# The end of a chunked scan: the last gate projection is moved ahead, output-projection units fill between the last head's steps, and its copies go to ScalarE

## What is computed

```python
def hgrn2_mixer(h, s0, lb, w_in, b_f, g_norm_w, w_out):
    q, f, i, z = jnp.split(h @ w_in, ...)
    q = silu(q); f = lb + (1 - lb) * sigmoid(f + b_f)
    logf = log(f); k = 1 - f; v = i
    o, S = hgrn2_scan(q, k, v, logf, s0)      # S_t = diag(f_t) S_{t-1} + k_t v_t^T, o_t = S_t^T q_t
    o = rmsnorm(o, g_norm_w)                  # over the 256 values of a head
    y = (o * silu(z)) @ w_out                 # the output projection
    return y, S
# and around it: x = x + gate * y
```

## Time and profile before

| | us |
|---|---|
| median of 3 runs | 1130.75 |
| lowest, highest | 1126.59, 1130.91 |
| profiled execution, its own time | 1128.67 |
| its span, first to last instruction | 1127.1 |
| PE busy | 1090.7 (97%) |
| DVE, ACT busy | 633.3 (56%), 506.0 (45%) |

### The profile page before, as it was taken

One profiled execution on the slowest core, in us unless ns is written; L12 is line 12 of the kernel. 1 busy time (PEld: TensorE's weight loads), 2 busy tenths in 40 slices (PEclk: granted clock), 3 DMA queues, 4 the chain that ended last, 5 costly groups with the idle time before them and its releaser, 6 DMA issues.

```text
span 1127.1 us, 26213 instructions
## 1 busy us (share of the span) xinstructions
PE 1090.7 (97%) x11141; PEld 1041.8 (92%) x11141; DVE 633.3 (56%) x1278; ACT 506.0 (45%) x1026; POOL 151.0 (13%) x156
## 2 busy tenths in 40 slices
PE   8999999999999999889998999999999999999998
PEld 6799999999999999779997999999999999998997
DVE  4776675858585758683435734552465246437332
ACT  4653444535444444641113554563465265447122
POOL 1000000000000000000000640252045006300000
PEclk9999999999999999999998999999999999999999
DMA  9864445444453535226224346424723652262541
GB/s 325 285 195 126 144 130 153 127 144 136 134 149 120 151 118 151 80 70 207 76 75 140 99 124 154 111 72 112 181 79 89 154 141 76 63 155 77 161 116 43
DMA packets 232218, 147.73 MB, mean 131 GB/s; under 512 B 7875, under 2 KB 226205, under 8 KB 231590
## 3 DMA queue, kind: packets, MB, share of 16 engines
q1 hardware_dynamic: 217456, 134.17, 41.9%
q10 hardware_dynamic: 14646, 11.89, 3.1%
HBM read 124.00 MB, written 22.02 MB: 130 GB/s over the span
## 4 chain that ended last, share of the span: by engine, by line
PE 79%; DVE 11%; ACT 4%; issue 3%; DMA 2%; SPq 1%; DVEq 0%; ACTq 0%
PE PJ L380 26%; PE PJ L1576 18%; PE PJ L1291 15%; PE PJ L401 2%; DVE dd L952 2%; PE X L1692 1%; PE X L1269 1%; PE X L1164 1%; PE PJ L1601 1%; PE X L1719 1%; PE PJ L624 1%; DVE atd L922 1%; PE X L1271 1%; DMA pre<-in_ada_w_dram 1%; PE X L1192 1%
## 5 line engine op out<-in xcount | busy, mean ns | idle before, releaser
L353 DVE TENSOR_TENSOR w_lo<-raw,w_hi 128x1024 fp32r<-128x1024 f32 (+1 forms) x128 | 157.0, 1240 | 178.8 <-ACT w_hi L345 169.9
L345 ACT ACTIVATE w_hi<-raw 128x1024 fp32r<-128x1024 f32 (+1 forms) x128 | 129.2, 1025 | 155.3 <-PE PJ L1576 69.9
L1576 PE MATMUL PJ<-w_hi,h_hi 128*128 128x256 f32 x600 | 167.3, 287 | 0.7 <-DVE w_lo L353 0.7
L1576 PE MATMUL PJ<-w_lo,h_hi 128*128 128x256 f32 x600 | 164.6, 283 | 0.0
L380 PE MATMUL PJ<-h_hi,w_hi 128*128 128x288 f32 (+1 forms) x736 | 160.7, 300 | 0.6 <-ACT v_ L874 0.6
L380 PE MATMUL PJ<-h_hi,w_lo 128*128 128x288 f32 (+1 forms) x736 | 157.7, 296 | 0.0
L380 PE MATMUL PJ<-h_lo,w_hi 128*128 128x288 f32 (+1 forms) x736 | 157.4, 295 | 0.0
L1576 PE MATMUL PJ<-w_hi,h_lo 128*128 128x256 f32 x480 | 135.8, 283 | 0.0
L380 PEld LDWEIGHTS PJ<-h_hi,w_hi 128*128 128x128 f32 x736 | 118.1, 189 | 4.3 <-issue 2.8
L380 PEld LDWEIGHTS PJ<-h_hi,w_lo 128*128 128x128 f32 x736 | 118.9, 189 | 0.0
L380 PEld LDWEIGHTS PJ<-h_lo,w_hi 128*128 128x128 f32 x736 | 118.8, 189 | 0.0
(11 more groups left out here) (329 smaller groups left out, 2165.7 us busy)
## 6 DMA issues: line engine op xcount, KB each, us to landing
raw<-in_a_w_in_dram SPq DMA_DIRECT2D x48, 512.0 KB, 4.9
raw<-in_ada_w_dram SPq DMA_DIRECT2D x32, 512.0 KB, 3.8
raw<-in_b_w_in_dram SPq DMA_DIRECT2D x64, 256.0 KB, 3.6
kvc<-in_cache_kv_w_dram SPq DMA_DIRECT2D x24, 512.0 KB, 5.8
pre<-in_ada_w_dram SPq DMA_DIRECT2D x16, 512.0 KB, 10.0
s<-in_state_hgrn_dram SPq DMA_DIRECT2D x8, 1024.0 KB, 8.4
out_hgrn_sample_dram<-s ACTq DMA_DIRECT2D x8, 1024.0 KB, 5.0
raw<-in_a_w_out_dram SPq DMA_DIRECT2D x16, 512.0 KB, 4.7
```

What stands on the lines that cost most here:

```text
L345: act.activation(w_hi[:, i % SPLITS, 0:size], raw[:, n % RAWS, 0:size], ACT.Copy).then_inc(hi_done, 1)
L353: dve.tensor_tensor(w_lo[:, i % SPLITS, 0:size], raw[:, n % RAWS, 0:size], w_hi[:, i % SPLITS, 0:size].bitcast(F32), ALU.subtract).then_in ...
L1576: last = pe.matmul(PJ[:, tile // 2, tile % 2 * 256:tile % 2 * 256 + 256], a, b[:, k, :], start=(first and k == 0 and i == 0), stop=(kk == ...
```

## The change

It touches heads 0 to 6 only in how waits and reads are worded (`pe_states` is cut into `pe_seq_rows`, `pe_chunk_states` and `pe_seq_out`, in the same order; some waits ask for less). The rest is at the end of the scan:

- PE, step 7: `project_T(ticket_w(7, 5), ...)` runs whole, after the new states and ahead of the output products of head 6.
- PE, step 8: the turning of the conditioning rows comes first, then units 0 and 1, `pe_mean(6)`, and units 2 to 7 one by one between the scan's parts. The chunk states come ahead of the sequences' rows.
- PE, step 9: units 8 and 9 ahead of `pe_mean(7)`, units 10 to 13 behind it, then units 0 to 7 of output block 1, then units 14 and 15 of block 0, and units 8 to 15 of block 1.
- ACT takes over eight copies of the last head (`at` from `X` and from `atd`, `sc`), under the new counter `at_done`. Its `oz_hi` copies are spread over steps 7, 8 and 9, and the `split_hi` of the three first output pieces is moved: two into step 7, ("out0", 1, 0) to the very end of step 8.
- DVE: the `oz_lo` are spread likewise, and the `split_lo` of ("out0", 1, 0) stands at the end of step 8, ahead of `oz_lo(8, 14)` of step 9.
- The transposed keys of the short sequences of the last head go to bank 2 of `X` in place of bank 1.

```diff
@@ act_step
             if h == AH:
-                for key in FIRST_OUT0[0:2]:
-                    split_hi(key)
+                oz_hi(4, 6)
             if end:
-                logs_and_exps()
+                if h <= AH:
+                    logs_and_exps()
...
             if h == AH:
-                z_sigmoid(AH - 1, 1)
-                split_hi(FIRST_OUT0[2])
-                oz_hi(0, 10)
+                oz_hi(6, 8)
+                act.wait_ge(gram_ready, 3 * g + 3)
+                act.wait_ge(op_ready, g)
+                for i in (6, 7):
+                    for s0_, s1_, t0_, t1_ in level_blocks(i):
+                        ins = act.activation(at[s0_:s1_, :, t0_:t1_], wide_at(i)[s0_:s1_], ACT.Copy)
+                ins.then_inc(at_done, 1)
...
+                if h == AH:
+                    act.wait_ge(up_ready, g + 1)
+                    act.wait_ge(sp_out, 16 * g)
+                    act.activation(sc[:, 0], X[:, 0, 0:ADV], ACT.Copy).then_inc(at_done, 1)
...
-                for j in range(2 if h < AH - 1 else 1):
+                for j in range(2):
                     z_sigmoid(h, j)
                     ahead(7 + j)
+                    if h == AH - 1 and j == 0:
+                        for key in FIRST_OUT0[0:2]:
+                            split_hi(key)
+            if h == AH - 1:
+                oz_hi(0, 4)
             if h == AH:
-                oz_hi(10, 14)
+                act.wait_ge(gram_read, 3 * g + 2)
+                for q in range(4):
+                    r = slice(BL * q, BL * q + BL)
+                    ins = act.activation(at[r, :, r], atd[r, 0:CH], ACT.Copy)
+                ins.then_inc(at_done, 1)
+                oz_hi(8, 10)
...
                 act.activation(sq0[:, :, TP:T], os_[:], ACT.Square).then_inc(sq_done, 1)
+                if h == AH:
+                    oz_hi(10, 14)
+                    split_hi(FIRST_OUT0[2])
@@ dve_step
             if h == AH:
-                for key in FIRST_OUT0[0:2]:
-                    split_lo(key)
+                z_gate(AH - 1, 1)
+                oz_lo(0, 4)
+                read_ada_chunk(chain, 3 + h)
+                oz_lo(4, 6)
             if h > AH:
-                oz_lo(4, 13)
+                oz_lo(8, 14)
...
-            if h == AH:
-                z_gate(AH - 1, 1)
-                split_lo(FIRST_OUT0[2])
             if h > AH:
-                oz_lo(13, 16)
+                oz_lo(14, 16)
...
             if scan and not new:
                 gram()
                 gram()
-                oz_lo(0, 2)
-                read_ada_chunk(chain, 3 + h)
                 masked_keys()
-                oz_lo(2, 4)
...
+            if h == AH:
+                oz_lo(6, 8)
...
                 new_states((0, 1), ub_read)
+            if h == AH - 1:
+                for key in FIRST_OUT0[0:2]:
+                    split_lo(key)
+            if h == AH:
+                split_lo(FIRST_OUT0[2])
@@ pe_step
             if h == AH:
-                late = (ticket_w(AH - 1, 5), ("w", AH - 1, 5))
-                project_T(*late, range(0, 4))
+                wait_read(pe, ticket_w(AH - 1, 5))
+                turn_ada_groups(3 + h)
+                out0_units(2)
                 pe_mean(pe, f)
-                project_T(*late, range(4, KD))
+                out0_units(3)
+                pe_grams(pe, g, 0)
+                out0_units(4)
+                pe_grams(pe, g, 1)
+                pe_grams(pe, g, 2)
+                out0_units(5)
+                pe_turn_keys(pe, g)
+                out0_units(6)
+                pe_chunk_states(pe, g)
+                pe_seq_rows(pe, g)
+                out0_units(7)
+                pe_seq_out(pe, g)
             if h > AH:
-                out0_units(4)
+                out0_units(10)
                 pe_mean(pe, f)
+                out0_units(14)
+                pe.wait_ge(ada_done, 4 + AH)
+                pe_out(pe, "out0", 1, range(8))
...
             if new:
                 pe.wait_ge(adr_done, 5 + h)
-                if h < AH - 1:
-                    project_T(ticket_w(h, 5), ("w", h, 5))
+                project_T(ticket_w(h, 5), ("w", h, 5), range(KD))
             elif scan:
-                out0_units(2)
+                out0_units(8)
             if scan:
                 pe.wait_ge(ua_read, g + 1)
+                if h == AH:
+                    pe.wait_ge(at_done, 3)
@@ the PE program, after the steps
             out0_units(16)
-            pe.wait_ge(ada_done, 4 + AH)
             for m in range(1, KD):
-                pe_out(pe, "out0", m, range(16))
+                pe_out(pe, "out0", m, range(8 if m == 1 else 0, 16))
```

More of the change, by code:

```diff
@@ L928, in dve_gram @@
                     dve.wait_ge(op_ready, g)
-                for q in range(4):
-                    r = slice(BL * q, BL * q + BL)
-                    dve.tensor_copy(at[r, :, r], atd[r, 0:CH])
+                if g < AH - 1:
+                    for q in range(4):
+                        r = slice(BL * q, BL * q + BL)
+                        dve.tensor_copy(at[r, :, r], atd[r, 0:CH])
                 for x in range(2):
                     r = slice(BL * x, BL * x + BL)
-                    dve.tensor_copy(atz[r, x], atd[r, CH])
-                for i in (6, 7):
+                    ins = dve.tensor_copy(atz[r, x], atd[r, CH])
+                for i in (6, 7) if g < AH - 1 else ():
                     for s0_, s1_, t0_, t1_ in level_blocks(i):
@@ L1048, in dve_step @@
                     dve.wait_ge(sp_out, 16 * g)
-                chain(dve.tensor_copy(sc[:, 0], X[:, 0, 0:ADV]))
+                if h < AH:
+                    chain(dve.tensor_copy(sc[:, 0], X[:, 0, 0:ADV]))
+                else:
+                    dve.wait_ge(at_done, 2)
                 for c in range(1, CH):
@@ L1119, in pe_grams @@
             if group == 2 and g >= 1:
-                pe.wait_ge(fin_done, 2 * g)
+                pe.wait_ge(fin_done, 2 * g - 1)
             for i in range(3 * group, min(3 * group + 3, 8)):
@@ L1138, in pe_turn_keys, with pe_turn_seq_keys, seq_keys_at, pe_seq_rows @@
         def pe_turn_keys(pe, g):
-            pe.wait_ge(gram_read, 3 * g + 3)
             pe.wait_ge(lv_done, XS * g + XS)
+            if g:
+                pe.wait_ge(fin_done, 2 * g)
             for c in range(CH):
                 pe.transpose(X[:, 3, c * P:(c + 1) * P], kh[:, c * P:(c + 1) * P], ident[:])
-            pe.transpose(X[:, 1, 0:P], kh[:, TP:T + TS], ident[:]).then_inc(kt_ready, 1)
-        def pe_states(pe, g):
+            pe_turn_seq_keys(pe, g)
+        def pe_turn_seq_keys(pe, g):
+            bank, c0 = seq_keys_at(g)
+            if g < AH - 1:
+                pe.wait_ge(gram_read, 3 * g + 2)
+            else:
+                pe.wait_ge(at_done, 1)
+            pe.transpose(X[:, bank, c0:c0 + P], kh[:, TP:T + TS], ident[:]).then_inc(kt_ready, 1)
+        def seq_keys_at(g):
+            return (1, 0) if g < AH - 1 else (2, 384)
+        def pe_seq_rows(pe, g):
             b = g % 2
+            pe.wait_ge(gram_read, 3 * g + 3)
+            if g == AH - 1:
+                pe.wait_ge(kz_done, g + 1)
             pe.wait_ge(vs_done, g + 1)
@@ L1234, in pe_step @@
                              lambda c: PJ[:, c // 2, c % 2 * ADV:(c % 2 + 1) * ADV], between)
-            elif h == AH:
-                grams(0)
-                grams(1)
-                wait_read(pe, ticket_w(AH - 1, 5))
-                turn_ada_groups(3 + h)
-                grams(2)
-            if scan:
-                if new:
-                    pe.wait_ge(ada_done, 4 + h)
+            if scan and new:
+                pe.wait_ge(ada_done, 4 + h)
                 pe_turn_keys(pe, g)
@@ L1247, in pe_step @@
                 project_ada(19 + 4 * h, 3)
-            if scan:
-                pe_states(pe, g)
+            if scan and new:
+                pe_seq_rows(pe, g)
+                pe_chunk_states(pe, g)
+                pe_seq_out(pe, g)
             if new:
@@ L1255, in pe_step @@
                 pe.wait_ge(up_read, g + 1)
-                pe.wait_ge(vs_done, g + 1)
+                pe.wait_ge(kz_done, g + 1)
                 pe_new_states(pe, g)
```

13 lines of the change are left out of this document (10 added, 3 removed).

## The result

| | before | after |
|---|---|---|
| median of 5 runs, us | 1130.75 | 1136.42 |
| lowest, highest | 1126.59, 1131.21 | 1135.22, 1136.93 |
| profiled execution, its own time | 1128.67 | 1136.00 |
| its span | 1127.1 | 1134.4 |

The ratio of after to before is 1.0052, with a 95% interval of 1.0035 to 1.0070. The change makes the kernel slower by half a percent; the 0.5% within which I had called two times the same lies inside the interval. Between the two profiled executions it is 7.3 us.

The account below looks back on a forecast made before the run. PE, 97% busy, was taken as bound at the scan's end by the chain through the parked input's read. PE resuming at 522.5 against 515.4, plus 1.8 clock, adds 8.9 to 1128.67: 1137.6, given as 1137.5 us, range 1131.0 to 1141.5.

Parts of the forecast that it names:

- issue gap: PE's unexplained stop within the last head's small matmuls: 2.24 us before, 1.4 us left with one unit put in between.
- wait ahead of unit 6: PE waits some 1.4 us for DVE's low part of block 6, made behind the chain for the new states.
- from there to unit 8: From PE issuing its last output product to unit 8: 7.0 us of squares, copies and splits in series on ACT and DVE.
- clock's price, first gap: Behind the gap between products and unit 8, PE runs at the lower clock: 1.59 to 2.3 us, taken as 1.8.
- from read to PE: From the start of the read of the parked input to PE resuming: 11.5 us, as in the trace of before.
- PE's wait there: Ahead of block 1's second half, PE waits 5.7 us, where it waited 0.69 us before.
- clock's price, second gap: Behind PE's wait ahead of block 1's second half, the clock falls again and costs 1.8 us.
- The stall: Between the products and unit 8, PE has nothing else to do for 7.0 us, which delays the read.
- In-order engines: ACT and DVE take instructions strictly in order, so low parts of blocks 8 and 9 can't pass the waiting piece.
- Heads 0 to 6: These heads gain 0, as none of their reworded waits stood in a gap.
- first rival: PE isn't held behind the products: resumes at 512.3, 1125.6 to 1127.4 us, say 1126.5; chance 0.11.
- third rival: All gaps close and the read costs nothing: 11 us gained, 1117.5 us; chance 0.05.

Follow-up runs that it names:

- e1_split_early: Changed kernel with the high and low part of piece (out0, 1, 0) made in the middle of step 8, not behind the products: 1128.49 us.
- e5_before_lo_early: Kernel before with DVE's wait for the read put behind the low part of piece (out0, 1, 1): 1130.61 us.
- e4_projection_alone: Kernel before with only the last gate projection, its sigmoid and gate moved whole into step 7: 1131.92 us.
- e2_fill_gap: Changed kernel with 48 matmuls of unused results on PE between the last head's products and unit 8: 1135.33 us.
- e3_lo_before_read: Changed kernel with DVE's wait for the read put behind the low part of piece (out0, 1, 1): 1133.50 us.
- e7_two_of_three: Changed kernel with piece (out0, 1, 0) split early and DVE's wait for the read behind the low part of (out0, 1, 1): 1125.53 us.
- e9_no_unit_between: Changed kernel with unit 3 moved from between the last head's first two groups of small matmuls to behind both: 1138.35 us, one run.
- e10_more_order: Changed kernel: e7_two_of_three's edits, units 14 and 15 inside block 1, units 3 and 4 between small-matmul groups, DVE's low parts of blocks 6 and 7 earlier: 1120.37 us.

## Why the prediction was right

The forecast was 1137.5 us, with a shift of 8.9 us on the profiled execution; the measured median is 1136.42 and the shift between the profiled executions 7.3 us. By its steps:

| step | said | measured |
|---|---|---|
| small matmuls start | 472.9 | 472.82 |
| issue gap | 1.4 | 1.26 |
| wait ahead of unit 6 | 1.4 | 1.37 |
| products issued | 493.0 | 493.2 |
| from there to unit 8 | 7.0 | 6.9 |
| unit 8 starts | 500.0 | 500.11 |
| clock's price, first gap | 1.8 | 1.34 |
| read starts | 511.0 | 510.63 |
| from read to PE | 11.5 | 10.17 |
| second half of block 1 | 522.5 | 520.80 |
| PE's wait there | 5.7 | 4.14 |
| clock's price, second gap | 1.8 | 1.2 |

**The stall** is the forecast's main step, and it holds in kind and size: e1_split_early takes it away by moving nothing but the piece. **In-order engines**: DVE's `w_lo` stood in front of `oz_low` and nothing passed it, though the inputs of two blocks were ready (489.46) and DVE was idle for 6.55 us. The rule that I had weighed against the trace says just this, that VectorE takes its instructions strictly in order (the Trainium skill, TensorE: Matmul & The Clock Gate, section Architectural detail: the array is 16× 32×32, not 1× 128×128); by that rule, the trace agrees, with 6.71 us. **Heads 0 to 6** got nothing, as said: the last matmuls ahead of the first changed place start at 456.64, against 456.63. **The issue gap**: the step 2.24 - 0.8 = 1.4 is right in kind, but that it came out at 1.26 is partly luck. The same order of matmuls gave 0.98 us in three of six traces, and with no unit in between it was 2.24, 1.88 and 1.37 us in before, e5_before_lo_early and e4_projection_alone.

**The absolute number** is nearer than the shift. The forecast added 8.9 us to the profiled execution of before, which was 2.1 us under the median; the medians differ by 5.7 us only, and the profiled executions by 7.3. That 1137.5 came within 1.1 us of 1136.42 owes that much to the base.

Three terms were too large, and together make up the 2.3 us by which the shift at the end of block 1 fell short (the sum for the residual starts at 528.55, against 521.91: 6.6 us, for 8.9; the other 0.7 us between the profiled executions came later and isn't explained). The read and what follows it took 10.17 us, since the read itself was 8.81 us and not the 10.16 of the earlier trace rows; I had taken one transfer's time as if it couldn't vary. The first clock's price was taken between 1.59 and 2.3 us and is 1.34 (e2_fill_gap), as only 3.02 us were run at the lower level; in e3_lo_before_read it was 0.8 us more behind the same gap, so the term varies between executions as the read does. The second: eight units take 528.55 - 520.80 = 7.75 us against 521.91 - 515.40 = 6.51, 1.2 us.

**What I had not seen.** That the second gap has two owners. I wrote that the high part of ("out0", 1, 1) "comes in time", which is true of after (516.75, with the read landing at 519.4) but hid that without the read 2.5 us would remain (e3_lo_before_read, e7_two_of_three): the change had put all of PE's cover ahead of the end of block 0. The first rival is what e1_split_early made: I had PE resume at 512.3 there, and it did at 512.26. But that is luck: the read started at 502.15 and not at 500.8 (the issue gap had stayed, with 0.98 us), and PE resumed 10.1 us later and not 11.5. The time was 1128.49 (1127.08 in the profiled execution) and not 1126.5; the clock's price, 1.5 us here, had gone into it only by half. The third rival I gave 0.05, since it "needs the read to be off the chain"; it couldn't be had by this change, but three moves more came nearer to its 1117.5, with 1121.74, and two further ones with 1120.37.

## What to carry to other kernels

Where engines work in order, a preparation step is harmless only where nothing behind it is urgent: look in each engine's queue at what stands ahead of the first instruction that the busiest engine will wait for, and add up that series. A gap that is closed is worth only what the chain of waits lets through; find the one event that the next long transfer hangs on, and do nothing ahead of it that can be done during the transfer. And when fillers are moved ahead of a gap, ask what they had covered where they stood: the projection covered two waits, and block 1's first half a split.

## What the runs showed of the hardware

**The clock behind a gap isn't the same from one execution to the next.** After a gap of 2.11 us in identical code, the granted clock was 0.53 in one execution and 1.00 in another (e5_before_lo_early). After 2.54 us, again the same gap, the first two matmuls took 0.85 us in e7_two_of_three (low) and 0.53 us in e3_lo_before_read. In e7_two_of_three it also fell at 487, behind waits of no more than 1.37 us, where e1_split_early with the same order has 1.00. After the gaps of 3.9 to 6.7 us it was always low. A forecast should hold the price of a short gap's clock as a range from nothing. It also goes with the spread of before: of its 60 executions taken beside the experiments, the 23 with a mean granted clock of at least 0.994 took 1126.4 to 1129.6 us, the other 37 took 1129.3 to 1133.8.

**A run of small matmuls stops once, and both the place and the end of the stop are nearly fixed.** Each head has 224 of them; in the last head's, PE stops once with no semaphore behind it:

| run | units among them | matmuls up to the stop | first one at | goes on at | distance | gap |
|---|---|---|---|---|---|---|
| before | 0 | 201 | 473.34 | 477.50 | 4.16 | 2.24 |
| e5_before_lo_early | 0 | 201 | 471.47 | 475.26 | 3.79 | 1.88 |
| e4_projection_alone | 0 | 201 | 473.39 | 477.28 | 3.89 | 1.37 |
| e9_no_unit_between | 0 | 171 | 473.11 | 476.83 | 3.72 | 2.06 |
| after | 1 | 165 + 6 | 472.82 | 476.82 | 4.00 | 1.26 |
| e1_split_early | 1 | 165 + 6 | 472.81 | 476.53 | 3.72 | 0.98 |
| e10_more_order | 2 | 159 + 12 | 473.17 | 476.89 | 3.72 | 0.23 |

In all three orders of the changed kernel the stop comes behind the same matmul of the stream, the 171st if those of the units are counted, and in all runs PE goes on 3.7 to 4.2 us behind the first one, whatever stands in between. So a unit put among them doesn't shorten a wait; it is work done while PE would have stood still, up to about two units. Each trace also shows one packet of 16 KB in the instruction queue (q8) some 1.2 to 1.6 us behind the first small matmul; whether PE waits for it wasn't tried, and why heads 0 to 6 have no such stop stays open.

**The same read took 8.5 to 10.2 us.** 10.2 us in before, 9.3 and 9.4 us in e5_before_lo_early and e4_projection_alone, and 8.5 to 8.8 us in after and its variants, with the same loads issued behind it. Why stays open.
